# Latent attention with the keys on the partitions: maxima from a pass of rounded products, sums by additions and ones, products of 512 queries

## What is computed

```python
def mla_block(q_nope, q_pe, k_nope, k_pe, v):
    scale = (C_NOPE + C_ROPE) ** -0.5
    s = (jnp.einsum('bhqd,bhkd->bhqk', q_nope, k_nope)
         + jnp.einsum('bhqr,bkr->bhqk', q_pe, k_pe)).astype(jnp.float32) * scale
    p = jax.nn.softmax(s, axis=-1)
    return jnp.einsum('bhqk,bhkd->bhqd', p.astype(v.dtype), v)
```

## Time and profile before

| | us |
|---|---|
| median of 3 runs (3263.05 to 3264.11) | 3263.72 |
| the profiled execution | 3261.77 |
| its span, first to last instruction | 3260.0 |
| TensorE busy, share of the span | 3131.0, 96% |
| VectorE busy | 2105.9, 65% |
| ScalarE busy | 1454.0, 45% |

### The profile page before, as it was taken

One profiled execution on the slowest core, in us unless ns is written; L12 is line 12 of the kernel. 1 busy time (PEld: TensorE's weight loads), 2 busy tenths in 40 slices (PEclk: granted clock), 3 DMA queues, 4 the chain that ended last, 5 costly groups with the idle time before them and its releaser, 6 DMA issues. The chain is left out here.

```text
span 3260.0 us, 48920 instructions
## 1 busy us (share of the span) xinstructions
PE 3131.0 (96%) x19182; PEld 2704.9 (83%) x19182; DVE 2105.9 (65%) x2520; ACT 1454.0 (45%) x2491; POOL 662.4 (20%) x776
## 2 busy tenths in 40 slices
PE   7999899899999999999998999999999999999997
PEld 5888777788999999988797778888887788888875
DVE  4999766555856556688644336555564676676877
ACT  5222456566323333444665325555554443333544
POOL 0001000121222222233022101111111223333323
PEclk8999999899999999999999999999999999999998
DMA  7224686533122122576734742422222232222765
GB/s 218 71 89 139 212 256 212 199 102 87 56 78 70 64 78 64 183 213 201 242 130 155 252 151 45 114 49 62 49 45 72 84 85 81 81 84 73 246 213 195
DMA packets 283859, 415.83 MB, mean 128 GB/s; under 512 B 90216, under 2 KB 188200, under 8 KB 282608
## 3 DMA queue, kind: packets, MB, share of 16 engines
q1 hardware_dynamic: 270256, 363.02, 36.2%
q0 software_dynamic: 13376, 49.69, 4.1%
HBM read 318.49 MB, written 94.13 MB: 127 GB/s over the span
## 5 line engine op out<-in xcount | busy, mean ns | idle before, releaser
L2160 DVE TENSOR_TENSOR ring_lo<-raw_rows,ring_hi 128x512 fp32r<-128x512 f32 x200 | 179.8, 900 | 203.9 <-ACT ring_hi L2011 203.5
L1283 PE MATMUL banks<-y_hi,ring_hi 128*128 128x384 f32 (+2 forms) x688 | 221.2, 322 | 4.9 <-DVEq L2148 4.1
L1285 PE MATMUL banks<-y_hi,ring_lo 128*128 128x384 f32 (+2 forms) x688 | 221.3, 322 | 0.0
L1284 PE MATMUL banks<-y_lo,ring_hi 128*128 128x384 f32 (+2 forms) x688 | 221.1, 321 | 0.0
L4609 DVE TENSOR_REDUCE mla_neg_max<-mla_scores 128x1 f32<-128x1280 f32 x128 | 190.3, 1487 | 46.9 <-PE mla_scores L90 46.9
L4579 ACT ACTIVATE mla_e<-mla_scores,mla_neg_max 128x1280 f32<-128x1280 f32 x128 | 170.1, 1329 | 110.8 <-DVE mla_neg_max L4609 110.8
L4521 PE MATMUL mla_turned<-ident,mla_e 128*128 128x128 f32 x1280 | 207.1, 276 | 1.9 <-ACT mla_pt L4587 1.3
L4521 PEld LDWEIGHTS mla_turned<-ident,mla_e 128*128 128x128 f32 x1280 | 157.0, 141 | 48.7 <-issue 12.2
L1283 PE MATMUL banks<-differences,ring_hi 128*128 128x512 f32 (+2 forms) x560 | 192.6, 344 | 3.4 <-ACT sums L2021 2.6
L1284 PE MATMUL banks<-differences,ring_hi 128*128 128x512 f32 (+2 forms) x560 | 192.5, 344 | 0.0
L1285 PE MATMUL banks<-differences,ring_lo 128*128 128x512 f32 (+2 forms) x560 | 192.5, 344 | 0.0
(11 more groups left out here) (541 smaller groups left out, 9087.3 us busy)
## 6 DMA issues: line engine op xcount, KB each, us to landing
raw_rows<-in_ffn_w_up SPq DMA_DIRECT2D x88, 512.0 KB, 3.6
da_ada_w<-in_ada_w SPq DMA_DIRECT2D x10, 4096.0 KB, 14.4
raw_rows<-in_ffn_w_down SPq DMA_DIRECT2D x110, 256.0 KB, 2.9
raw_rows<-in_ffn_w_down SPq DMA_DIRECT2D x44, 512.0 KB, 4.5
out_raw<-scratch_act SPq DMA_DIRECT2D x66, 256.0 KB, 3.5
sums<-scratch_act SPq DMA_DIRECT2D x55, 256.0 KB, 3.4
ab_raw<-in_ab_w_in SPq DMA_DIRECT2D x20, 512.0 KB, 4.2
scratch_act<-conv_lines SPq DMA_DIRECT2D x20, 512.0 KB, 4.8
```

The costliest lines, as they stand in the source:

```text
L1283: pe.matmul(out, w_hi[:, w], b_hi[:, a:a + n], start=start and k == 0, stop=False, skip_group_check=True)
L1284: pe.matmul(out, w_hi[:, w], b_lo[:, a:a + n], start=False, stop=False, skip_group_check=True)
L1285: mm = pe.matmul(out, w_lo[:, w], b_hi[:, a:a + n], start=False, stop=k == KD // 2 - 1, skip_group_check=True)
L2160: dve.tensor_tensor(blocks(begun.lo(r)), source(r), blocks(begun.hi(r)).bitcast(F32), ALU.subtract)\
```

## The change

Scores are now computed with the keys on the partitions: a tile of 128 keys x 512 queries, 20 to a head (`scores`), so that the exponentials need no transpose before the products with the values (`product`, 512 queries wide). The softmax's maxima, which are now needed along the partitions, come from a pass of their own: `piece` multiplies only the hi parts with the queries on the partitions, VectorE reduces them (`smallest`, ten reductions a head), and the negated maxima go through eight transfers (`shift_row`) into a 97th row of the queries, which meets a row of ones in the keys; so the scores come out shifted. Sums over the keys are made by VectorE adding the tiles of exponentials (`add`) and by TensorE with ones (`total`); VectorE inverts a whole bank (`inverse`), scales (`scale`) and takes the rest (`rest_out`); GpSimd has nothing left but three fills at the start. The pass for head h+1 is woven into head h. The loads of a head still wait for the last score of two heads before; hi parts come first. The eight loads of output weights are spread, one in each of the heads 4 to 11.

The added lines of its core (removed ones are those printed above):

```diff
+def load_part(sp, h, part, q, k, q_parts, k_parts, signal):
+    sp.dma_start(k[0:C_NOPE, :].bitcast(F32), k_parts[part][h * C_NOPE:(h + 1) * C_NOPE, :]).then_inc(signal, 16)
+    sp.dma_start(q[0:C_NOPE, :].bitcast(F32), q_parts[part][h * C_NOPE:(h + 1) * C_NOPE, :]).then_inc(signal, 16)
+    first = C_HEADS * C_NOPE + h * C_ROPE
+    sp.dma_start(q[C_NOPE:C_NOPE + C_ROPE, :].bitcast(F32), q_parts[part][first:first + C_ROPE, :]).then_inc(signal, 16)
...
+    E_SLOTS = 7
+    FILLS = 2 * KT + 1
+    SUM_AT = 5
+    MAIN, TAIL = 2 * BANK, T - 2 * BANK
+    ADDS = KT - 2
...
+    order = [(0, 0), (1, 0), (0, 1), (1, 1)] + [(kt, c) for kt in range(2, KT) for c in range(2)]
+    pieces = [("main", 0), ("main", 1), ("main", 2), ("main", 3), ("tail", 0),
+              ("main", 4), ("main", 5), ("main", 6), ("main", 7), ("tail", 1)]
+    piece_at = {2: 0, 4: 1, 5: 2, 7: 3, 8: 4, 10: 5, 11: 6, 13: 7, 14: 8, 15: 9}
...
+            def shift_row(h, c):
+                sp.wait_ge(s.shifted.sem, 2 * h + c + 1)
+                half = XT // 2
+                src = shift[:, h % 2, c * half:(c + 1) * half].bitcast(F32)
+                dst = qs[h % 2][0][HD:HD + 1, c * BANK:(c + 1) * BANK].bitcast(F32)
+                for t in range(half):
+                    sp.dma_start(dst[:, t * P:(t + 1) * P], src[:, t:t + 1], allow_slow_non_contiguous=True)\
+                      .then_inc(row_in[c].sem, 16)
...
+            sp.wait_ge(s.set.sem, 3)
+            one, zero = acc[0:1, :, :].rearrange("p a n -> p (a n)"), e[0:1, 0:2, :].rearrange("p a n -> p (a n)")
+            for q, k in zip(qs, ks):
+                sp.dma_start(k[0][HD:HD + 1, :].bitcast(F32), one[:, 0:T]).then_inc(s.unit_in.sem, 16)
+                sp.dma_start(k[1][HD:HD + 1, :].bitcast(F32), zero[:, 0:T]).then_inc(s.unit_in.sem, 16)
...
+            shift_row(0, 0)
+            shift_row(0, 1)
+            for h in range(1, H):
+                if h >= 2:
+                    head(h)
+                    values(h)
+                shift_row(h, 0)
+                shift_row(h, 1)
+                if 4 <= h < 4 + KD:
+                    k = h - 4
+                    sp.dma_start(w_raw[:, k, :], w_out[k * P:(k + 1) * P, :]).then_inc(s.w_in.sem, 16)
...
+            def slot_free(f):
+                h, at = divmod(f - 3, FILLS)
+                if f < 3 or (at == SUM_AT and h == 0):
                     return
...
+                if at == SUM_AT:
+                    pe.wait_ge(s.inverted.sem, h)
+                else:
+                    pe.wait_ge(s.exp.sem, min(2 * KT * h + at + 1 - (at > SUM_AT), 2 * KT * H))
...
+            def piece(h, n):
+                kind, t = pieces[n]
+                if n == 0:
+                    if h == 0:
                         pe.wait_ge(first_in, 16 * FIRST_LOADS)
...
+                    else:
+                        pe.wait_ge(hi_in[h % 2].sem, 16 * PART_LOADS * ((h + 1) // 2))
+                    if h == 1:
+                        pe.wait_ge(s.pe_in.sem, 32)
+                index = len(pieces) * h + n
+                if index >= 2:
+                    pe.wait_ge(s.piece_least.sem, index - 1)
+                q, k, out = qs[h % 2][0], ks[h % 2][0], m_ps[:, index % 2, :]
+                if kind == "main":
+                    for a in range(0, MAIN, BANK):
+                        mm = pe.matmul(out[:, a:a + BANK], q[0:HD, t * P:(t + 1) * P], k[0:HD, a:a + BANK],
+                                       start=True, stop=True)
+                else:
+                    for j in range(XT // 2):
+                        tokens = slice((4 * t + j) * P, (4 * t + j + 1) * P)
+                        mm = pe.matmul(out[:, j * TAIL:(j + 1) * TAIL], q[0:HD, tokens], k[0:HD, MAIN:T],
+                                       start=True, stop=True)
+                mm.then_inc(s.piece_full.sem, 1)
...
+            def scores(h, i):
+                kt, c = order[i]
+                if i == 0:
+                    if h == 0:
+                        pe.wait_ge(s.unit_in.sem, 16 * UNIT_LOADS)
+                    else:
+                        pe.wait_ge(lo_in[h % 2].sem, 16 * PART_LOADS * ((h + 1) // 2))
+                if kt == 0:
+                    pe.wait_ge(row_in[c].sem, 16 * XT // 2 * (h + 1))
+                f = score_fill(h, i)
...
+                exact_product(pe, s_ps[:, f % 3, :], k_hi[:, keys], k_lo[:, keys], q_hi[:, tokens], q_lo[:, tokens],
+                              True, True).then_inc(s.s_full.sem, 1)
...
+            def product(h, kt):
+                pe.wait_ge(s.exp.sem, exps_of(h, kt))
+                if kt == 0:
                     pe.wait_ge(v_in[h % 2].sem, 16 * (h // 2 + 1))
...
+                    pe.wait_ge(s.o_copied.sem, h)
+                for c in range(2):
+                    mm = pe.matmul(o_ps[c * C_V:(c + 1) * C_V, :], v[:, h % 2, kt, :],
+                                   e[:, (h * KT + kt) % E_SLOTS, c * BANK:(c + 1) * BANK], start=kt == 0, stop=kt == KT - 1)
+                mm.then_inc(s.o_step.sem, 1)
+            def total(h):
+                f = sum_fill(h)
+                slot_free(f)
+                if h == 0:
+                    pe.wait_ge(s.set.sem, 3)
+                pe.wait_ge(s.added.sem, ADDS * (h + 1))
+                for c in range(2):
+                    tokens = slice(c * BANK, (c + 1) * BANK)
+                    pe.matmul(s_ps[c * C_V:(c + 1) * C_V, f % 3, :], ones[:, :], acc[:, h % 2, tokens],
+                              start=True, stop=False)
+                for c in range(2):
+                    tokens = slice(c * BANK, (c + 1) * BANK)
+                    mm = pe.matmul(s_ps[c * C_V:(c + 1) * C_V, f % 3, :], ones[:, :],
+                                   e[:, (h * KT + KT - 1) % E_SLOTS, tokens], start=False, stop=True)
+                mm.then_inc(s.sum_full.sem, 1)
...
+            for n in range(len(pieces)):
+                piece(0, n)
+            for h in range(H):
+                for i in range(2 * KT):
+                    scores(h, i)
+                    if i == 1 and h:
+                        product(h - 1, KT - 1)
+                    if i >= 3 and i % 2:
+                        product(h, (i - 3) // 2)
+                    if i == SUM_AT - 1 and h:
+                        total(h - 1)
+                    if i in piece_at and h + 1 < H:
+                        piece(h + 1, piece_at[i])
+            product(H - 1, KT - 1)
+            total(H - 1)
+            hold_clock(pe, m_ps[:, 0, 0:P], ident[:, :], 20)
...
+            def smallest(h, n):
+                kind, t = pieces[n]
+                index = len(pieces) * h + n
+                dve.wait_ge(s.piece_full.sem, index + 1)
+                src = m_ps[:, index % 2, :]
+                if kind == "main":
+                    dve.tensor_reduce(least[:, 0, t:t + 1], src, AX.X, ALU.max, negate=True).then_inc(s.piece_least.sem, 1)
                     return
...
+                at = slice(t * XT // 2, (t + 1) * XT // 2)
+                dve.tensor_reduce(least[:, 1, at], src.rearrange("p (t n) -> p t n", n=TAIL), AX.X, ALU.max, negate=True)\
+                   .then_inc(s.piece_least.sem, 1)
+                dve.wait_ge(s.piece_least.sem, index + 1)
+                dve.tensor_tensor(shift[:, h % 2, at], least[:, 0, at], least[:, 1, at], ALU.min).then_inc(s.shifted.sem, 1)
...
+            def inverse(h):
+                dve.wait_ge(s.sum_full.sem, h + 1)
+                dve.wait_ge(s.scaled.sem, h)
+                dve.reciprocal(inv, s_ps[:, sum_fill(h) % 3, :]).then_inc(s.inverted.sem, 1)
...
+            for h in range(H):
+                def following(*which):
+                    for n in which:
+                        if h + 1 < H:
+                            smallest(h + 1, n)
+                if h:
+                    add(h - 1, 7)
+                    add(h - 1, 8)
+                following(0)
+                if h:
+                    inverse(h - 1)
+                following(1)
+                if h:
+                    scale(h - 1)
+                following(2, 3)
+                add(h, 1)
+                following(4)
+                add(h, 2)
+                following(5, 6)
+                add(h, 3)
+                following(7, 8, 9)
+                for kt in range(4, 7):
+                    add(h, kt)
+                if h and h % 2 == 0:
+                    rest_out(h // 2 - 1)
+            add(H - 1, 7)
+            add(H - 1, 8)
+            inverse(H - 1)
+            scale(H - 1)
+            rest_out(H // 2 - 1)
...
+            pool.memset(ones[:, :], 1.0).then_inc(s.set.sem, 1)
+            pool.memset(acc[0:1, :, :], 1.0).then_inc(s.set.sem, 1)
+            pool.memset(e[0:1, 0:2, :], 0.0).then_inc(s.set.sem, 1)
```

More of the change, by code:

```diff
@@ L4528, in product @@
-            def product(pair):
-                f = product_fill(pair)
-                h = pair // PER_HEAD
-                bank_free(f)
-                vector, scalar = copies(2 * pair + 1, 2)
```

(62 more changed lines are left out.)

245 lines of the change are left out of this document (56 added, 189 removed).

## The result

The changed kernel takes 3339.5 us (median of four runs, 3337.2 to 3348.0), the kernel before 3263.4 beside it (3260.7 to 3264.1): a ratio of 1.0239, interval 1.0221 to 1.0258. It is slower by 76 us where 41 were forecast, inside the range. The stage takes 616.6 us (1944.1 to 2560.7) instead of 544.8, so 72 of the 76 us are in it.

A forecast was written before the change was run, and what follows sets the result against it. TensorE's queue was taken to bound the stage: start 21.0, first head 28.3, 14 heads 483.0, output weights 10.4, last head 26.8, end 11.4, clock 5 make 586 against 544.8. That is 41 us more: 3305 us, range 3270 to 3345.

The forecast's parts named there:

- TensorE's work per head: Latent attention stage: scores, rounded products, products with the values and sums take 31.4 us a head, against 33.2 before.
- The wait for hi parts with the output weights: Head boundaries: TensorE waits 2.0 us for loads in 14 heads, 1.3 more in eight with output weights.
- The clock: After long waits TensorE drops to 1.2 GHz, costing 1.7 us each time; three drops counted, 5 us.
- Rival D: Waits at head boundaries drop the clock in every head: 24 us instead of 5, 3324; chance 0.15.
- The wait behind the reciprocal: Fifth rounded piece: TensorE waits 1.1 us for its buffer, since VectorE's reciprocal precedes later reductions; in 14 heads.
- the reciprocal's price: VectorE's reciprocal of a 128x512 bank, once a head: 3.2 us, from the slope of small operations.
- Start: Stage's start: first exact scores at 21.0 us, the row of maxima being queued behind the loads.
- End: Stage's end: last product, sums, reciprocal, scaling, rounding, rest, latencies and barrier take 11.4 us.
- A: Hi parts land within 4.3 us and product pieces cost 1.0: 40 us less, 3224; chance 0.06.
- B: The row of maxima's eight transfers take 10 us and hold the next head, 4 us in 15 heads: 3365; chance 0.12.
- C: VectorE's reciprocal runs at 0.7 us, no wait for piece 5: 18 us less, 3287; chance 0.2.
- E: No difference: boundary costs are half (wait 1.0, no weights' delay, start 15), 3265; chance 0.04.

The follow-up runs named there:

- e_order: Changed kernel with the next head's rounded products starting after the fifth triple of scores, not the third, and VectorE's reciprocal ahead of the first two reductions: 3276.6 us.
- e_third2: Changed kernel with a third buffer for the hi parts of queries and keys, so that they are loaded a head earlier: 3289.9 us.
- e_recip: Changed kernel with VectorE copying the sums instead of taking their reciprocal, so outputs are not divided by the right number: 3324.4 us.
- e_best: e_order plus product pieces in pairs, and the first head's row of maxima issued ahead of the second head's lo parts and values: 3247.7 us.
- e_hold: Changed kernel with ten unread fp32 products of the identity ahead of TensorE's wait for hi parts in heads 2 to 15: 3331.2 us.
- e_pair: Changed kernel with the product pieces in pairs after every fourth triple of scores, instead of one after every second: 3327.1 us.
- e_best2: e_best with the sums' products directly ahead of the first product pair, and the first rounded piece ahead of the sums: 3266.3 us.
- e_best3: e_best with the sums directly ahead of the first product pair, and the first rounded piece behind both: 3257.7 us.
- e_order_pair: e_order with the product pieces in pairs and nothing else, the start as in the changed kernel: 3253.4 us.

## Why the prediction was right, and where its sizes were off

The direction, the place and the mechanism were right: a head that costs TensorE no less than before once the rounded pass, the sums and the changes of width are paid; a wait for hi parts in 14 heads; a start of over 20 us. The stage was forecast at 586 and took 616.6. By its terms:

- TensorE's work per head: 31.4 forecast, 32.75 by e_order, where TensorE waits for nothing. Mis-sized by 1.35 x 16 = 22 us. The ten product pieces, "1.0 to 1.15, and I take 1.1", are 1.2 each (1.0 a head), above my bound; the rest is 0.1 for the sums and 0.01 for each triple. Its reason, a change of width of about 0.25, is 0.30 to 0.35: the lead in, and the first product behind it.
- The wait for hi parts with the output weights: 38.4 forecast (2.0 a head, 3.3 with a load of weights); TensorE was idle for 1.1 to 1.9 us a head and for 2.7 to 3.2 with such a load, 32 in all, and the gaps, counted from 0.23 us after the start of the triple's last pass to the start of the rounded piece, add up to 34.3.
- The clock: "I count three", 5 us. Mis-sized, and the larger error for its size: 41 us at half clock cost 20.5, and the first head began with 5.3 us more of it, 2.6. Rival D described it; I gave it 0.15 although the wait that I forecast myself, 2.0 to 3.3 us in every head, was longer than the only one that I knew to be followed by a drop (1.3 us in the earlier trace rows). 18 us.
- The wait behind the reciprocal: 1.1 x 14 = 15.4 forecast; 4.0 of idle time measured, 6.2 in gaps counted in the same way, 9 too much. VectorE's timetable came as forecast. In the thirteenth head, from its first score at 2414.57, the reciprocal runs from 9.9 to 13.2 and the third reduction ends at 17.0 (10.0, 13.2 and 17.2 forecast). But TensorE, whose work behind the sums is longer than forecast, comes to the fifth rounded piece at 16.5, not at 16.2, and starts it at 17.0: the gap is 0.56 us there and about 0.3 in every other head, not 1.1. It isn't that the wait for loads covers this one: e_third2 has neither that wait nor slow stretches, and waits 0.4 us for the same minima. The lines of the thirteenth head (the second one holds the third and the fourth reduction):

```profile
2424.43 3.36 DVE L4668 RECIPROCAL w_first<-mla_scores 128x512 f32<-128x512 f32 x1 [3.25 <-PE mla_scores L4581]
2430.31 2.35 DVE L4645 TENSOR_REDUCE mla_least<-mla_rounded 128x1 f32<-128x1024 f32 x2
2430.80 0.39 PE L90 MATMUL mla_scores<-q_first_hi,k_first_lo 97*128 97x512 f32 x1
2431.59 0.74 PE L4539 MATMUL mla_rounded<-mla_k_hi,mla_q_hi 96*128 96x256 f32 x4 [0.41 <-DVE mla_least L4645]
```

  By these lines the term is small; e_recip's medians, 15 us apart, leave room for 8 us more. That the reciprocal's price was within 5% is partly luck: it came from one difference of 12 ns, between a reciprocal of two elements and another operation of one, taken as the price of both elements.
- Start 21.0, measured 24.4: the eight issues of the row took 7.2 us, 0.9 each, and landed behind the loads of the second head. End 11.4, about 12.

22 - 4.1 + 18 - 9.2 + 3.4 + 0.6 = 31, against 30.6; 4 us more lie outside the stage, which no run explains. That the time stayed inside the range, 5.5 us below its upper end, is owed to errors of both signs. The rivals: A needed loads within 4.3 us and pieces of 1.0; neither came. e_best, without the wait and with 1.03 us a piece in pairs, has the sign that A had, at 31.0 instead of 30.4 us a head. B fell: the eight transfers of the second head landed 1.9 to 2.0 us after their issue (from 1986 on), and TensorE waits for none but the first head's. C fell by the reciprocal's duration; its price, 18 us, is near the 15 that e_recip gained. E fell: the wait was 1.4 us on average without output weights, not 1.0, these weights delayed the loads by 1.5, and the start took 24.4 instead of 15.

That the clock falls because of these waits is shown by e_hold, where only the idle time was filled, and by e_third2, where the wait was taken away. Why e_pair has 6.8 us of it in every head and the changed kernel mostly 3.4 was only seen, not tested.

## What to carry to other kernels

When a change puts a load's landing between two heads, add up the work that TensorE still has there against the landing time first: here 4.3 us against 6.3 by the forecast decided 50 us (e_third2). Two changes of order did it without another buffer: the next pass started two triples later and the long VectorE operation came first, 63 us less than the changed kernel (e_order). Price a wait together with the clock behind it, and measure an edit of TensorE's order only once such waits are gone, since until then the clock takes back what it gains (the pairs gave 12 us with the wait, 23 without it). Keep products of one width together, at 0.35 us a change, and look at what the new order makes the other engines late for: in e_best2 and e_best3 that cost more than the change saved.

## What the runs showed of the chip that I had not expected

- In the middle of the stage the slow stretches come in 3.4 or 6.8 us (at its start they last 20 to 31), and their sum differs with the schedule, in the one profiled run of each: 41 us in the changed kernel, 85 with shorter heads and the same wait, 3.4 with the idle time filled, none between the second head and the last but one in e_third2, e_order, e_order_pair and e_best, which there wait for 0.4 us or less at a time.
- A change of width is paid at three places. The timeline of e_best around a pair:

```profile
2187.19 0.39 PE L90 MATMUL mla_scores<-mla_q_hi,mla_k_lo 97*128 97x512 f32 x1
2187.51 1.94 PE L4566 MATMUL mla_out<-mla_e,ckv 128*64 128x512 f32 x8
2189.38 0.73 PE L4535 MATMUL mla_rounded<-k_first_hi,q_first_hi 96*128 96x512 f32 x2
2189.94 0.40 PE L88 MATMUL mla_scores<-mla_q_hi,mla_k_hi 97*128 97x512 f32 x1
```

  0.09 ahead, 1.87 for both pieces, 0.10 in the products behind: 2.06 us, where two pieces apart cost 2.4.
- Eight small transfers of 512 bytes take mostly 0.6 us each to issue, but one took 2.2 while larger loads were under way (at 1960.3); issued ahead of those loads they landed sooner. First the changed kernel's row of these transfers (KB each, median us to landing), from 1957.2 to 1965:

```profile
q_first_hi<-mla_shift SPq DMA_DIRECT2D x8, 0.5 KB, 7.7
```

and that of e_best, from 1944 to 1960:

```profile
q_first_hi<-mla_shift SPq DMA_DIRECT2D x8, 0.5 KB, 4.1
```
